# Eighteen ring places for expert weights, two of them shared with the routing tables, in a two-layer decoder step

## The chip, the cores and the metric

The kernel runs on one core of one Trainium2 chip. The metric is the device time of one launch in microseconds; the kernel before has a median of 1427.11 us over 3 runs (1426.06 to 1427.96). All data is float32.

## The reference, cut to what matters

A decoder step of two layers over 512 prompt tokens and 8 sample tokens (520 rows of 1024 elements). Layer 0 attends by stick-breaking, layer 1 by dilated windows over a shared K/V. Each layer ends with the same mixture of experts:

```
def hmoe(h, w_rg, b_rg, w_re, b_re, w_g, w_u, w_d):
    g_idx  = argmax(softmax(h @ w_rg + b_rg))            # one of 4 groups
    top_i  = top_k(softmax(logits of the 8 experts of that group), 2)
    comb   = weights of the two chosen experts, over all 32
    a, u   = einsum('td,edf->tef', h, w_g), einsum('td,edf->tef', h, w_u)
    return einsum('tef,efd->td', silu(a) * u * comb[:, :, None], w_d)
```

Each of the 32 experts has a gate and an up matrix of 1024 x 256 and a down matrix of 256 x 1024, 1 MiB each: 96 matrices, 100.7 MB, in each layer. A token uses two experts, and the kernel reads every expert's weights once per layer.

## The kernel before, in words

The stages follow one another as blocks, in which each engine has its own instruction list and the engines meet through semaphores: attention of layer 0, `moe(0)`, `layer_b` (attention of layer 1: projections from three weight units per key head, then scores, softmax and products), a last stage for the sample rows, `moe(1)`, and a block that adds the experts' rows and stores the output.

**A mixture stage.** TensorE turns the rows of x and multiplies them with the router. VectorE works out the first and second choice of every token, the rank of each token within its expert, and the tables of rows (`lg`, `el`, `tmp`, `run`, `own`, `at`, `who` and others, lines 960 to 990). TensorE reduces the tables to row numbers (semaphore `s_tab`), VectorE writes them to `idx` (L1363), and GpSimd gathers the rows of two experts at a time from DRAM into `xs` (L1464). Beside it VectorE counts tokens beyond the 64 places of an expert and signals `s_over` (L1390); such an overflow has a path of its own after the last pair, which uses some of the tables again. Then come 16 pairs of experts. For each, TensorE multiplies with gate and up (L1034), turns h (L1043, L1045) and multiplies with down (L1052); ScalarE and VectorE copy the results to `ysb`, and GpSimd scatters them to `y_rows` in DRAM (L1470).

**The ring.** A weight matrix is a piece of 1 MiB, 8 KiB on each partition. The pieces are numbered in the order of use: gate and up of expert 2v, gate and up of 2v+1, then the two downs, six for a pair v. They go round a ring of 16 places: the 12 homes of the buffer `slots`, in the order `HOME = (7, 8, ..., 11, 0, ..., 6)`, then two halves of `spare`, `gain_rows`, and a part of `oT`. SyncE (SP) asks for them in its list, L330. The first 12 are asked for as the homes come free, some at the end of the stage before (`load_first`), pieces 12 to 15 after the normed rows are stored and the router is done. From piece 16 on, piece n waits in `used(n - 16)` until TensorE has signalled that the piece which had its place is used.

**After the ring.** In layer 0, SP then asks for the gains `gcol` and for the three weight units of key head 0 of `layer_b` (`load_unit`, L349 to L351): for each unit two parts of 256 KB, in runs of 256 bytes, and one of 1 MB, in runs of 1 KiB, 1.57 MB in all. A unit lies in `slots` from element 14400 on, over homes 7 to 11; `unit_pieces(g)` names the last pieces that used them. All engines leave the stage when SP has seen all scatters landed (`all_stored`).

**The start of `layer_b`.** `rows_back(sp, 0)` and `rows_back(act, 1)` read the 520 rows of the first and of the second choice back from `y_rows` (L1612, 2.13 MB on the queue of SP and as much on that of ScalarE). SP then asks for the head gains `gn` (L1676, L1677). VectorE's list is: clear `tok` (L1979), scale unit 0 by its gains (L1994), ten additions into x, two for each of the five row tiles (L1984), wait for `gn`, two instructions on the gains (L2115, L2116), evict the first two products of unit 0 (L2013, L2014), scale unit 1, and so on; unit 2 is scaled after the second product of unit 1. TensorE warms up (`keep_busy`, L215), turns tile 0 of x when its two additions are done (L1718), multiplies it with unit 0 (L1734), turns tiles 1 and 2, multiplies tile 1, turns tiles 3 and 4, and multiplies tiles 2 and on. The product of tile 2 waits until that of tile 0 has been evicted, since there are two banks.

Of the kernel before, what the change touches and what calls it, by code (L numbers as in the profile page):

```python
# [1 line left out]

# [12 lines left out]
D = 1024  # L15
# [4 lines left out]
NT = len(TILES)  # L20
# [10 lines left out]
NDIL = 3  # L31
KQ = 5 * HD
NG, NE, EPG = 4, 32, 8
FE = D // 4
CAP = 64
NOVER = 2 * TOK // CAP
# [93 lines left out]
def flat(ap):  # L130
    return ap.rearrange("p a b -> p (a b)")


def build(nc, a, outs):
# [11 lines left out]
    with ExitStack() as ctx:  # L146
        def sb(name, shape, dt=F32, to=ctx):
            return to.enter_context(nc.sbuf_tensor(name, shape, dt))
# [38 lines left out]
        gain_rows = sb("gain_rows", [128, 2, D])  # L187
# [111 lines left out]
        PIECE = 2 * D  # L299
        slots = sb("slots", [128, 12 * PIECE])  # L300

        RING = 16
        HOME = (7, 8, 9, 10, 11, 0, 1, 2, 3, 4, 5, 6)

        def home(i):
            return slots[:, PIECE * i:PIECE * i + PIECE]

        def piece(n):

            p, k = n // 6, n % 6  # L310
            return (2 * p + k // 2, k % 2) if k < 4 else (2 * p + k - 4, 2)
# [14 lines left out]
        def load_piece(eng, layer, n, dst):  # L326

            e, k = piece(n)
            sig = s_din[layer][e % 6] if k == 2 else s_gin[layer][e % 6]
            eng.dma_start(dst, weight_rows(layer, e, k)).then_inc(sig, 16)  # L330

        def load_first(eng, layer, homes):
            for i in homes:
                load_piece(eng, layer, HOME.index(i), home(i))

# [10 lines left out]
        def load_unit(sp, j, g):  # L346

            kv = [ds(g * 512 + which * 256 + j * HD, HD) for which in range(2)]
            sp.dma_start(wB[:, g, :, 0:HD], w_kv[:, :, kv[1]]).then_inc(s_unit[g], 16)  # L349
            sp.dma_start(wB[:, g, :, HD:2 * HD], w_kv[:, :, kv[0]]).then_inc(s_unit[g], 16)  # L350
            sp.dma_start(wB[:, g, :, 2 * HD:], w_q[:, :, ds(g * D + j * 256, 256)]).then_inc(s_unit[g], 16)  # L351

        def unit_pieces(g):

            lo, hi = WB + g * KT * UW, WB + (g + 1) * KT * UW
            return [3 * NE - RING + HOME.index(i) for i in range(lo // PIECE, -(-hi // PIECE))]

        phA = ExitStack()
        live.append([])
# [121 lines left out]
        with ExitStack() as ph, nc.Block() as block:  # L481
# [15 lines left out]
            spare = wA[:, 0].rearrange("p k n -> p (k n)")  # L497
# [434 lines left out]
        def moe(layer, norm):  # L932

            L = str(layer)

            def lsem(n):
                return sem(f"{n}_{L}")
# [5 lines left out]
            with ExitStack() as ph, nc.Block() as block:  # L943
                oT_flat = flat(oT)
# [3 lines left out]
                ysb = [sb(f"ysb{w}_" + L, [2 * CAP, D], to=ph) for w in range(2)]  # L948
                spare = sb("spare" + L, [128, 4, D], to=ph)
                xn = [spare[:, w, :] for w in range(NT - 2)] + ysb  # L950
                ring = [home(i) for i in HOME] + [flat(spare[:, 0:2]), flat(spare[:, 2:4]), flat(gain_rows), oT_flat[:, 0:2 * D]]
                over_w = [home(k) for k in range(3)]

                def gate_up_of(w):
# [2 lines left out]
                def down_of(w):  # L957
                    return w.rearrange("p (f d) -> p f d", f=2)

                lg = sb("lg" + L, [128, NT, NG + NE], to=ph)  # L960
                st = sb("st" + L, [128, 9, NT], to=ph)
                g4 = sb("g4" + L, [128, 3, NT, NG], to=ph)
                el = sb("el" + L, [128, NT, NE], to=ph)
                oh = sb("oh" + L, [128, 3, NT, NE], to=ph)
                tmp = sb("tmp" + L, [128, NT, NE], to=ph)
                run = sb("run" + L, [128, NT - 1, NE], to=ph)
                rank = sb("rank" + L, [128, NT * NE], to=ph)
                own = sb("own" + L, [128, 2, NT * NE], to=ph)
                place = sb("place" + L, [128, 2 * NT], to=ph)
                at = sb("at" + L, [128, 2 * NT, CAP], to=ph)  # L970
                who = sb("who" + L, [128, 2 * NT, 2, 2, NE // 2], to=ph)
                idx = sb("idx" + L, [128, 2, NE // 2], I32, to=ph)
                nov = sb("nov" + L, [NE, 2, 128], to=ph)
                ovb = sb("ovb" + L, [128, NE + 1], to=ph)
                far = sb("far" + L, [128, NE], to=ph)
                ovm = sb("ovm" + L, [1, NOVER, NE], to=ph)
                ovf = sb("ovf" + L, [1, NOVER + 1], to=ph)
                oblk = sb("oblk" + L, [128, 2 * NT, NOVER], to=ph)
                owho = sb("owho" + L, [128, 2 * NT, 2, NOVER], to=ph)
                otab = sb("otab" + L, [CAP, 2, NOVER], to=ph)  # L980
                turn_mark = sb("turn_mark" + L, [1, 4], to=ph)
                oidx = sb("oidx" + L, [CAP, 2], I32, to=ph)
# [4 lines left out]
                s_xn, s_tp, s_ev, s_l, s_ex, s_gx, s_oh, s_rk, s_at, s_tab, s_idx, s_nv, s_ob, s_over = (  # L987
                    lsem(n) for n in ("xn_ready", "xn_turned", "xnT_ready", "logits_done", "exp_in",
                                      "exp_ready", "onehot_ready", "ranks_done", "places_ready", "tables_done", "rows_known",
                                      "over_counted", "over_base", "over_known"))  # L990
# [3 lines left out]
                s_xs = [lsem(f"xs_in{w}") for w in range(2)]  # L994
# [101 lines left out]
                @block.sync  # L1096
                def _(sp):
                    open_ring(sp, s_ye + [o_dn, o_ye, o_free])
                    load_first(sp, layer, range(early, early + 2))
                    for t, rows in TILES:  # L1100
                        sp.wait_ge(s_xn, t + 1)
                        sp.dma_start(xn_rows[128 * t:128 * t + rows, :], xn[t][0:rows, :]).then_inc(s_st[0 if t < NT - 2 else NT - 2], 16)
                    load_first(sp, layer, range(early + 2, len(HOME)))
                    sp.wait_ge(s_st[0], 16 * (NT - 2))
                    load_piece(sp, layer, 12, ring[12])
                    load_piece(sp, layer, 13, ring[13])
                    if layer == 0:
                        sp.wait_ge(s_cleared, 16 * (-(-2 * TOK // 128)))
                    load_piece(sp, layer, 14, ring[14])
                    sp.wait_ge(s_l, NT)  # L1110
                    load_piece(sp, layer, 15, ring[15])

                    def used(n):
                        e, k = piece(n)
                        if k == 2:
                            sp.wait_ge(s_dn[e % 2], e // 2 + 1)
                        else:
                            sp.wait_ge(s_gu[e % 2], e // 2 + 1)

                    for n in range(RING, PIECES):  # L1120
                        used(n - RING)
                        load_piece(sp, layer, n, ring[n % RING])
                    if layer == 0:
                        sp.dma_start(gcol[:, 0], a["g_kv"].rearrange("(p t) -> p t", t=KT)).then_inc(s_gcol, 16)
                        sp.dma_start(gcol[:, 1], a["g_attn"][1].rearrange("(p t) -> p t", t=KT)).then_inc(s_gcol, 16)
                        for g in range(NDIL):
                            for n in unit_pieces(g):
                                used(n)
                            load_unit(sp, 0, g)

                    with further_blocks(sp, lambda: all_stored(sp)) as (m, _):
                        e = sp.value_load(over_i[0:1, ds(m, 1)], min_val=0, max_val=NE - 1)
                        sp.wait_ge(o_dn, m + 1)
                        for k in range(3):
                            sp.dma_start(over_w[k], weight_rows(layer, e, k)).then_inc(o_in, 16)
                    all_stored(sp)

                @block.tensor
                def _(pe):
# [56 lines left out]
                    def experts(v):  # L1196
                        n, b = v // 2, v % 2
                        pe.wait_ge(s_xe[b], 2 * n + 2)
                        for q in range(2):
                            e = 2 * v + q  # L1200
                            pe.wait_ge(s_gate_up_in[e % 6], 32 * (e // 6) + 32)
                            gate_up(pe, gate_up_of(ring[(6 * v + 2 * q) % RING]), gate_up_of(ring[(6 * v + 2 * q + 1) % RING]), q,
                                    xsT[b][:, :, CAP * q:CAP * q + CAP], s_gu[q])
# [7 lines left out]
                        for q in range(2):  # L1211
# [3 lines left out]
                            pe.wait_ge(s_down_in[e % 6], 16 * (e // 6) + 16)  # L1215
                            down(pe, down_of(ring[(6 * v + 4 + q) % RING]), q, s_dn[q])

# [333 lines left out]
        def layer_b(norm, next_norm):  # L1551
# [15 lines left out]
            with ExitStack() as ph, nc.Block() as block:  # L1567
# [41 lines left out]
                def rows_back(eng, k, some=TILES):  # L1609
                    for t, rows in some:  # L1610
                        r0 = TOK * k + 128 * t
                        eng.dma_start(yr[0:rows, 2 * t + k, :], y_rows[r0:r0 + rows, :]).then_inc(s_gt[t], 16)  # L1612
# [11 lines left out]
                def _(sp):  # L1624
# [48 lines left out]
                        sp.dma_start(dst[n1:n1 + n2 - 1, :, 1, :], rows("cache_kv_b3", 16)).then_inc(s_past[c], 16)  # L1673

                    rows_back(sp, 0)
                    sp.dma_start(gn[:, 0], a["k_norm_b"].partition_broadcast(128)).then_inc(s_gn, 16)  # L1676
                    sp.dma_start(gn[:, 1], a["q_norm_b"][0].partition_broadcast(128)).then_inc(s_gn, 16)  # L1677
                    sp.wait_ge(norm.s_rstd, NT)
# [812 lines left out]
```

## Time and profile before

| What | Value |
|---|---|
| median of 3 runs | 1427.11 us |
| the profiled execution, its own time | 1429.2 us |
| its span, first to last instruction | 1427.3 us |
| TensorE busy | 1298.7 us (91%) |
| VectorE / ScalarE / GpSimd busy | 44% / 23% / 31% |
| bytes moved by DMA | 319.90 MB, mean 224 GB/s |
| experts of layer 0, of layer 1 | about 385 to 617 us, 1164 to 1399 us |

A busy TensorE is not one at its peak: an instruction that follows closely behind another counts as busy, and `keep_busy` products count too. The page's slices are 35.7 us each. The stretches in which the DMA engines move some 420 GB/s are the two expert stages.

### The profile page before, as it was taken

The numbers are of one execution on the slowest core, as the hardware profiler recorded it, in microseconds if no ns is written. First come the engines' busy times: TensorE is split into PE (matmuls) and PEld (weight loads), VectorE is DVE, ScalarE is ACT, GpSimd is POOL, SyncE is SP. The second block draws the span as 40 slices with busy tenths as digits, with TensorE's granted clock in tenths as the row PEclk, the third lists the DMA queues.
The fourth block names the chain that finished last, engine by engine and source line by source line (L and its number), as shares of the span: only waits on it lengthen the run. The fifth ranks groups of instructions, "written<-read, shape, count | busy, mean of one in ns | idle before, by whom it ended". The sixth has DMA issues, their size and how long they took to land. (4 is left out here: it accounts for less than half of the span.)

```text
span 1427.3 us, 20804 instructions
## 1 busy us (share of the span) xinstructions
PE 1298.7 (91%) x8666; PEld 916.9 (64%) x8666; DVE 625.1 (44%) x940; ACT 323.8 (23%) x642; POOL 443.1 (31%) x381
## 2 busy tenths in 40 slices
PE   7889999999999988879999999999999989997882
PEld 5668878645666644537868868878746646664550
DVE  2277774633522111144457558558446542221114
ACT  3222223312122211112015015015015312221110
POOL 4122325201111111103977576577430101111100
PEclk9999999999999999999999999999999989999996
DMA  9944434263799999991222123022041869999995
GB/s 331 311 134 143 155 112 153 74 267 147 298 420 419 419 420 419 413 297 25 73 61 61 40 53 90 11 53 92 22 121 45 323 272 420 418 419 420 419 394 197
DMA packets 154864, 319.90 MB, mean 224 GB/s; under 512 B 63060, under 2 KB 112100, under 8 KB 130068
## 3 DMA queue, kind: packets, MB, share of 16 engines
q1 hardware_dynamic: 139764, 280.47, 52.6%
q0 software_dynamic: 13824, 33.84, 6.6%
q10 hardware_dynamic: 1184, 4.26, 0.8%
q8 instruction: 70, 1.15, 0.3%
q14 instruction: 22, 0.18, 0.0%
HBM read 300.71 MB, written 34.33 MB: 235 GB/s over the span
## 5 line engine op out<-in xcount | busy, mean ns | idle before, releaser
L1734 PE MATMUL ps<-slots 128*128 128x384 f32 x768 | 261.3, 494 | 0.9 <-ACT slots L1932 0.6
L1734 PEld LDWEIGHTS ps<-slots 128*128 128x128 f32 x768 | 203.1, 270 | 43.4 <-issue 3.0
L1034 PE MATMUL ps<-slots,oT 128*64 128x256 f32 x1536 | 179.8, 390 | 31.7 <-DMA slots<-in_w_up 30.2
L1034 PEld LDWEIGHTS ps<-slots,oT 128*64 128x64 f32 x1536 | 125.7, 140 | 92.0 <-issue 34.4
L583 PE MATMUL ps<-xnT_a,wA 128*128 128x260 f32 (+1 forms) x768 | 172.8, 385 | 3.2 <-DMA wA<-in_w_qkv_a 2.4
L583 PEld LDWEIGHTS ps<-xnT_a,wA 128*128 128x128 f32 x768 | 145.6, 191 | 28.4 <-issue 4.5
L1470 POOL DMA_INDIRECT y_rows<-ysb,idx x32 | 32.1, 1003 | 403.3 <-DVE ysb L1069 403.3
L1060 DVE TENSOR_TENSOR h<-sg,ps 64x256 f32<-64x256 f32 x64 | 26.4, 413 | 262.9 <-ACT sg L1057 262.9
L1052 PE MATMUL ps<-slots,hT 128*64 128x512 f32 x384 | 87.7, 597 | 2.3
L1069 DVE COPY ysb<-ps 64x512 f32<-64x512 f32 x64 | 44.4, 693 | 88.2 <-PE ps L1052 88.2
L1057 ACT ACTIVATE sg<-ps 64x256 f32<-64x256 f32 x64 | 24.4, 381 | 244.5 <-PE ps L1034 244.5
L1954 ACT ACTIVATE slots<-slots,neg 128x128 f32<-128x128 f32 (+1 forms) x192 | 64.1, 417 | 54.8 <-DVE neg L2057 49.2
L912 POOL TENSOR_TENSOR slots<-slots,cst 128x512 f32<-128x512 f32 x32 | 49.4, 1564 | 66.9 <-ACT slots L734 66.8
L891 POOL DMA_INDIRECT slots<-in_cache_kv_a,gidx x32 | 33.3, 1040 | 113.9 <-DVE gain_rows L798 104.4
L2218 POOL TENSOR_TENSOR late_b<-tok 128x1600 f32<-128x1600 f32 x12 | 34.2, 2853 | 105.4 <-DVE tok L2022 105.4
L829 DVE TENSOR_TENSOR_SCAN slots<-slots,gain_rows 128x1024 f32<-128x1024 f32 (+1 forms) x32 | 53.8, 1721 | 27.5 <-POOL slots L912 27.5
L1066 ACT ACTIVATE ysb<-ps 64x512 f32<-64x512 f32 x64 | 37.8, 590 | 108.0 <-PE ps L1052 108.0
L284 PE MATMUL ps<-slots,oT 128*128 128x512 f32 x128 | 58.2, 600 | 1.7 <-PEq L1567 1.3
L1052 PEld LDWEIGHTS ps<-slots,hT 128*64 128x64 f32 x384 | 30.3, 136 | 41.9 <-issue 41.9
L292 DVE TENSOR_TENSOR x<-x,ps 128x512 f32<-128x512 f32 x32 | 21.9, 687 | 77.9 <-PE ps L284 77.9
L2013 DVE TENSOR_SCALAR tok<-ps,rsr 128x320 f32<-128x320 f32 x32 | 17.6, 551 | 85.3 <-PE ps L1734 85.1
L2221 POOL TENSOR_TENSOR late_b<-late_b 128x800 f32<-128x800 f32 (+2 forms) x72 | 53.1, 737 | 5.7
(277 smaller groups left out, 1998.0 us busy)
## 6 DMA issues: line engine op xcount, KB each, us to landing
slots<-in_w_down SPq DMA_DIRECT2D x48, 1024.0 KB, 26.5
slots<-in_w_gate SPq DMA_DIRECT2D x48, 1024.0 KB, 23.2
slots<-in_w_up SPq DMA_DIRECT2D x48, 1024.0 KB, 27.1
wA<-in_w_qkv_a SPq DMA_DIRECT2D x24, 512.0 KB, 4.5
slots<-in_w_q_b SPq DMA_DIRECT2D x12, 1024.0 KB, 7.0
spare<-in_w_gate SPq DMA_DIRECT2D x8, 1024.0 KB, 23.3
spare<-in_w_up SPq DMA_DIRECT2D x8, 1024.0 KB, 26.9
gain_rows<-in_w_gate SPq DMA_DIRECT2D x8, 1024.0 KB, 21.1
```

What stands on the lines that cost most here:

```text
L284: last = nc.tensor.matmul(bank(at + n)[0:TILES[t][1], :], oT[:, m, 128 * t:128 * t + TILES[t][1]], self.w[m][:, 512 * n:512 * n + 512], st ...
L583: last = nc.tensor.matmul(bank(6 + h)[:, 0:half], wA[:, m, k, :], xnT[:, k, half * h:half * h + half], start=(k == 0), stop=(k == KT - 1))
L829: nc.vector.tensor_tensor_scan(P, P, keep[:, at:at + width][:, ::-1], 1.0, ALU.mult, ALU.add).then_inc(s_scan, 1)
L912: nc.gpsimd.tensor_tensor(d, d, C("below").unsqueeze(1).unsqueeze(1).to_broadcast([128, 2, 2, 128]), ALU.mult).then_inc(s_msk, 1)
L1034: last = nc.tensor.matmul(bank(q)[lo:lo + CAP, 0:FE], x[:, k, :], wt[:, k, :], start=(k == 0), stop=(k == KT - 1))
L1052: last = nc.tensor.matmul(bank(4 + q)[CAP * n:CAP * n + CAP, :], hT[:, q, f, :], wt[:, f, 512 * n:512 * n + 512], start=(f == 0), stop=(f ...
L1066: return nc.scalar.activation(ysb[w][CAP * q:CAP * q + CAP, 0:512], bank(4 + q)[0:CAP, :], ACT.Copy)
L1069: return nc.vector.tensor_copy(ysb[w][CAP * q:CAP * q + CAP, 512:D], bank(4 + q)[CAP:2 * CAP, :])
L1734: last = nc.tensor.matmul(bank(i % 2)[:, 0:UW], xT[:, kt, cols], wB[:, g, kt, :], start=(kt == 0), stop=(kt == KT - 1))
L1954: last = nc.scalar.activation(v, v, ACT.Exp, bias=neg[:, 0 if g else 1, b, h:h + 1])
L2218: pool_do(P.tensor_tensor(sq[:, :, :], kq, kq, ALU.mult))
L2221: pool_do(P.tensor_tensor(s4[:, :, :, 0:w], s4[:, :, :, 0:w], s4[:, :, :, w:2 * w], ALU.add))
```

## The change

The ring gets 18 places. The two new ones are the halves of a buffer `scratch` of 2 x 2048 elements per partition, from which a helper `table` cuts ten of the routing tables, which had buffers of their own. Piece 16 takes the first half, after the first gather has landed (`s_xs[0]`) and the tables are reduced (`s_tab`); piece 17 takes the second, after `s_over`. Piece n from 18 on waits for the use of piece n - 18. `HOME` becomes 0 to 11 in order. Unit 0 of `layer_b` is still asked for at the end of `moe(0)`; units 1 and 2 are asked for in `layer_b`, behind `rows_back(sp, 0)` and ahead of `gn`.

```
-        RING = 16
-        HOME = (7, 8, 9, 10, 11, 0, 1, 2, 3, 4, 5, 6)
+        RING = 18
+        HOME = tuple(range(12))
...
-            return [3 * NE - RING + HOME.index(i) for i in range(lo // PIECE, -(-hi // PIECE))]
+            return [max(range(HOME.index(i), 3 * NE, RING)) for i in range(lo // PIECE, -(-hi // PIECE))]
...
-                ring = [home(i) for i in HOME] + [flat(spare[:, 0:2]), flat(spare[:, 2:4]), flat(gain_rows), oT_flat[:, 0:2 * D]]
+                scratch = sb("scratch" + L, [128, 2, PIECE], to=ph)
+                ring = [home(i) for i in HOME] + [flat(spare[:, 0:2]), flat(spare[:, 2:4]), flat(gain_rows), oT_flat[:, 0:2 * D],
+                                                  scratch[:, 0], scratch[:, 1]]
+                def table(half, rows, *shape):      # the next free stretch of that half of scratch, in that shape
...
-                lg = sb("lg" + L, [128, NT, NG + NE], to=ph)
+                lg = table(0, 128, NT, NG + NE)
...              (so too el, tmp, run, at, who in half 0; own, nov, ovm, oblk, owho in half 1)
                     load_piece(sp, layer, 15, ring[15])
+                    sp.wait_ge(s_xs[0], 16)
+                    sp.wait_ge(s_tab, 1)
+                    load_piece(sp, layer, 16, ring[16])
+                    sp.wait_ge(s_over, 1)
+                    load_piece(sp, layer, 17, ring[17])
...
-                        for g in range(NDIL):
-                            for n in unit_pieces(g):
-                                used(n)
-                            load_unit(sp, 0, g)
+                        for n in unit_pieces(0):
+                            used(n)
+                        load_unit(sp, 0, 0)
...
                     rows_back(sp, 0)
+                    load_unit(sp, 0, 1)
+                    load_unit(sp, 0, 2)
                     sp.dma_start(gn[:, 0], a["k_norm_b"].partition_broadcast(128)).then_inc(s_gn, 16)
```

## Rows read from the trace of the kernel before

**Rows 1.** The page: span, and GB/s in 40 slices of it.
```profile
span 1427.3 us, 20804 instructions
...
GB/s 331 311 134 143 155 112 153 74 267 147 298 420 419 419 420 419 413 297 25 73 61 61 40 53 90 11 53 92 22 121 45 323 272 420 418 419 420 419 394 197
```

**Rows 2.** Windows: stretch, length, busy by engine, then PEclk, DMA share, GB/s.
```profile
390.00:604.00 214.00, 193.41 (x1395) 125.84 (x1393) 41.52 (x89) 45.04 (x89) 27.57 (x28) 0.99 1.01 417
1172.00:1386.00 214.00, 191.72 (x1381) 124.63 (x1378) 41.30 (x89) 44.90 (x89) 27.26 (x27) 0.99 1.01 419
384.00:390.00 6.00, 5.28 (x49) 3.60 (x49) 0.55 (x2) 2.75 (x4) 0.99 (x1) 1.00 0.18 51
1160.00:1170.00 10.00, 8.27 (x41) 5.37 (x43) 0.00 (x0) 2.48 (x3) 0.99 (x1) 0.54 0.11 30
```

**Rows 3.** Waits of TensorE, 460 to 620 us: total, times, longest, in us.
```profile
PE ps L1034 <- DMA slots<-in_w_up: 15.3, 10, 2.5
```

**Rows 4.** Timeline, layer 0, 383 to 403 us: start, duration, engine, line, what.
```profile
383.20 0.74 PE L1021 MATMUL ps<-cst,xs 128*128 128x128 f32 x2 [0.68 <-DMA xs<-xn_rows,idx]
...
383.97 0.17 DVE L1390 CAST over_i<-ovf 1x17 int32<-1x17 f32 x1
...
389.16 0.80 SPq L330 DMA_DIRECT2D slots<-in_w_down  x2
...
402.07 0.82 SPq L330 DMA_DIRECT2D slots<-in_w_down  x2
```

**Rows 5.** Timeline, layer 1, 1158 to 1171 us.
```profile
1158.34 0.16 DVE L1390 CAST over_i<-ovf 1x17 int32<-1x17 f32 x1
1161.04 0.56 PEld L1021 LDWEIGHTS ps<-cst,xs 128*128 128x128 f32 x2 [4.98 <-DMA xs<-xn_rows,idx]
...
1170.35 0.81 SPq L330 DMA_DIRECT2D slots<-in_w_down  x2
```

**Rows 6.** Timeline, end of `moe(0)` and start of `layer_b`, 595 to 655 us.
```profile
595.05 16.03 SPq L350 DMA_DIRECT2D slots<-in_w_kv_b  x1
...
607.93 3.67 PE L1034 MATMUL ps<-spare,oT 128*64 128x256 f32 x32 [1.19 <-DMA spare<-in_w_up]
...
618.25 0.97 POOL L1470 DMA_INDIRECT y_rows<-ysb,idx  x1 [13.54 <-DVE ysb L1069]
...
627.81 2.25 SPq L1612 DMA_DIRECT2D slots<-y_rows  x5
...
627.85 8.14 PE L215 MATMUL ps<-cst 128*128 128x512 f32 x12 [6.70 <-PEq L943]
...
629.17 3.42 DVE L1994 TENSOR_TENSOR slots<-slots,gcol 128x1024 f32<-128x1024 f32 x2
...
634.53 7.89 DVE L1984 SCALAR_TENSOR_TENSOR x<-slots,wts,x 128x1024 f32<-128x1024 f32 x6 [1.93 <-DMA slots<-y_rows]
...
637.19 1.16 PE L1718 MATMUL ps<-cst,x 128*128 128x128 f32 x8 [1.19 <-DVE x L1984]
...
642.88 5.22 DVE L1984 SCALAR_TENSOR_TENSOR x<-slots,wts,x 128x1024 f32<-128x1024 f32 x4 [0.47 <-DMA slots<-y_rows]
...
648.14 0.35 DVE L2115 TENSOR_SCALAR late_b<-late_b 128x192 f32<-128x192 f32 x1
...
649.25 0.55 DVE L2013 TENSOR_SCALAR tok<-ps,rs 128x320 f32<-128x320 f32 x1
649.72 0.28 DVE L2014 TENSOR_SCALAR vo<-ps,rs 128x64 f32<-128x64 f32 x1
...
654.17 10.59 PE L1734 MATMUL ps<-slots 128*128 128x384 f32 x32
```

**Rows 7.** Timeline, end of `moe(1)` and the last block.
```profile
1401.12 0.97 POOL L1470 DMA_INDIRECT y_rows<-ysb,idx  x1 [13.03 <-DVE ysb L1069]
1405.71 2.58 SPq L1523 DMA_DIRECT2D yr<-y_rows  x5
...
1410.70 7.89 DVE L1544 SCALAR_TENSOR_TENSOR x<-yr,wts,x 128x1024 f32<-128x1024 f32 x6 [10.41 <-DMA yr<-y_rows]
```

**Rows 8.** Windows around weight units, columns as in rows 2.
```profile
727.00:733.00 6.00, 6.00 (x32) 3.66 (x31) 2.26 (x4) 0.00 (x0) 5.61 (x6) 1.00 0.96 258
628.00:642.00 14.00, 12.46 (x30) 5.86 (x31) 11.74 (x9) 2.06 (x3) 1.39 (x2) 0.81 1.01 372
```

More of the change, by code:

```diff
@@ L1 @@
+import math
 from contextlib import ExitStack, contextmanager
@@ L950, in moe @@
                 xn = [spare[:, w, :] for w in range(NT - 2)] + ysb
-                ring = [home(i) for i in HOME] + [flat(spare[:, 0:2]), flat(spare[:, 2:4]), flat(gain_rows), oT_flat[:, 0:2 * D]]
+                scratch = sb("scratch" + L, [128, 2, PIECE], to=ph)
+                ring = [home(i) for i in HOME] + [flat(spare[:, 0:2]), flat(spare[:, 2:4]), flat(gain_rows), oT_flat[:, 0:2 * D],
+                                                  scratch[:, 0], scratch[:, 1]]
+                taken = [0, 0]
+                def table(half, rows, *shape):
+                    lo = taken[half]
+                    taken[half] = lo + math.prod(shape)
+                    assert taken[half] <= PIECE
+                    dims = "abcd"[:len(shape)]
+                    return scratch[0:rows, half, lo:taken[half]].rearrange(
+                        f"p ({' '.join(dims)}) -> p {' '.join(dims)}", **dict(zip(dims, shape)))
                 over_w = [home(k) for k in range(3)]
@@ L958, in down_of @@
                     return w.rearrange("p (f d) -> p f d", f=2)
-                lg = sb("lg" + L, [128, NT, NG + NE], to=ph)
+                lg = table(0, 128, NT, NG + NE)
                 st = sb("st" + L, [128, 9, NT], to=ph)
                 g4 = sb("g4" + L, [128, 3, NT, NG], to=ph)
-                el = sb("el" + L, [128, NT, NE], to=ph)
+                el = table(0, 128, NT, NE)
                 oh = sb("oh" + L, [128, 3, NT, NE], to=ph)
-                tmp = sb("tmp" + L, [128, NT, NE], to=ph)
-                run = sb("run" + L, [128, NT - 1, NE], to=ph)
+                tmp = table(0, 128, NT, NE)
+                run = table(0, 128, NT - 1, NE)
                 rank = sb("rank" + L, [128, NT * NE], to=ph)
-                own = sb("own" + L, [128, 2, NT * NE], to=ph)
+                own = table(1, 128, 2, NT * NE)
                 place = sb("place" + L, [128, 2 * NT], to=ph)
-                at = sb("at" + L, [128, 2 * NT, CAP], to=ph)
-                who = sb("who" + L, [128, 2 * NT, 2, 2, NE // 2], to=ph)
+                at = table(0, 128, 2 * NT, CAP)
+                who = table(0, 128, 2 * NT, 2, 2, NE // 2)
                 idx = sb("idx" + L, [128, 2, NE // 2], I32, to=ph)
-                nov = sb("nov" + L, [NE, 2, 128], to=ph)
+                nov = table(1, NE, 2, 128)
                 ovb = sb("ovb" + L, [128, NE + 1], to=ph)
                 far = sb("far" + L, [128, NE], to=ph)
-                ovm = sb("ovm" + L, [1, NOVER, NE], to=ph)
+                ovm = table(1, 1, NOVER, NE)
                 ovf = sb("ovf" + L, [1, NOVER + 1], to=ph)
-                oblk = sb("oblk" + L, [128, 2 * NT, NOVER], to=ph)
-                owho = sb("owho" + L, [128, 2 * NT, 2, NOVER], to=ph)
+                oblk = table(1, 128, 2 * NT, NOVER)
+                owho = table(1, 128, 2 * NT, 2, NOVER)
                 otab = sb("otab" + L, [CAP, 2, NOVER], to=ph)
```

## The prediction, made before the changed kernel was timed

> **What bounds the kernel now.** I read the page first, for where the DMA engines are full. The 40 slices show two stretches at 420 GB/s, slices 12 to 17 and 34 to 38, and mostly far less elsewhere [rows 1]. These are the two expert stages, and the reader is to see that they run at one rate whatever TensorE does. I then asked for windows: 417 and 419 GB/s at a share of 1.01 over 214 us in either layer, and ahead of each a hole, 51 GB/s between 384 and 390 us and 30 GB/s between 1160 and 1170 us [rows 2]. In the hole the ring is full: all 16 pieces have landed, and the next is asked for only when the first expert is done, at 389.16 us [rows 4] and at 1170.35 us [rows 5].
>
> TensorE would be faster than the DMA. While it still lives on the pieces in stock, the wait for the same place of the pair is passed 12.91 us apart (389.16 and 402.07 us [rows 4]). Six pieces are 6.29 MB, at 417 GB/s 15.1 us. So the stock of 16 runs out, and from 460 us on TensorE waits for up matrices, 15.3 us in ten waits on those in `slots` alone [rows 3], the last one at 607.93 us, for the very last gate and up pair [rows 6]. An expert stage therefore ends at: the moment the DMA begins again after the hole, plus the bytes still to come, plus a tail of fixed work. I looked last at that tail, in the timeline of both layers [rows 6, 7], because the change moves DMAs out of it in one layer, and the other shows it without them.
>
> **The ring, in both layers.** Piece 16 may now go when the first gather has landed and the tables are reduced. TensorE starts on that gather's rows at 383.20 us [rows 4] and at 1161.04 us [rows 5]. Piece 17 may go after the overflow count, 383.97 plus 0.17 us [rows 4] and 1158.34 plus 0.16 us [rows 5]. Both conditions come before the first expert is done, by 5 us in layer 0 and by 9 us in layer 1. Two pieces take 2 x 1.049 MB / 417 GB/s = 5.0 us, so they just fit the hole of layer 0 and easily that of layer 1. At 389.16 us SP asks for pieces 18 and 19 where it asked for 16 and 17, and so on: each request goes out when it did before and is for a piece two further on. The saturated stretch has 78 pieces to bring in place of 80, the same gathers and scatters, and ends 5.0 us sooner. Layer 0: -5.0 us. Layer 1: -5.0 us.
>
> Does TensorE become the bound before that? Its waits for weights add up to over 15 us [rows 3], of which 5 go, and the last wait is at the end of the stretch, so the DMA still decides. The bounds of this term: -5.4 us for a layer, if the DMA also starts sooner by what is left of the gap, and -2.5 us, if only one piece fits in the hole.
>
> The Trainium skill ("DMA: Bandwidth & Descriptors", Specifications) gives about 358 GB/s as the limit of HBM for one core. By it two pieces would be worth 5.9 us a layer; the 417 and 419 GB/s of rows 2 speak against it here, and the sum goes by these.
>
> The tables' move to `scratch` changes no shape of a VectorE or TensorE instruction; I cost it at nothing. The order of `HOME` decides which of the first pieces comes first; all 16 are in before the first expert starts, since the DMA is idle by then [rows 2], so it costs nothing either. The two new waits of SP stand in front of `used(0)`, and are over before it, as shown; behind them SP has only weight requests.
>
> **The end of `moe(0)`.** The last scatter goes out at 618.25 us, and all engines go on at 627.81 us, 9.56 us later [rows 6]. In layer 1, with no weight units behind the experts, it is 1401.12 to 1405.71 us, 4.59 us [rows 7]. In between SP asks in layer 0 for units 1 and 2, whose 3.1 MB share the DMA engines with the scatter. After the change only unit 0 is left. Its first parts were blocked in SP's queue for 16.03 us, until 611.08 us, when the weights had nearly all landed [rows 6]; that block moves along with the weights, so unit 0 should be in when the scatter starts or shortly after. I take the value of layer 1: -5.0 us. Bounds: 0 (unit 0 disturbs the scatter as all three did) and -5.0 us.
>
> **The rows back.** VectorE is free for the additions 4.8 us after the stage's start S (629.17 + 3.42 - 627.81 [rows 6]); its first addition starts at S + 6.72 us, waiting for rows, while the same rows are there at S + 4.99 us in layer 1 [rows 7]. Behind the change no rest of unit 2 is in the queue ahead of the rows. -1.7 us (bounds 0 and -1.9, where VectorE itself is the bound). TensorE turns tile 0 at S + 9.38 us now, after two additions of 1.32 us (7.89 / 6 [rows 6]); then at 5.0 + 2.6 = S + 7.65 us. Its warm-up of 12 products takes 8.14 us here, after 6.70 us of idle time [rows 6], and the granted clock of these 14 us is 0.81 in the mean [rows 8], so some 5 us at 1.2 GHz and the rest at 2.4; that idle time shrinks to 1.7 us, so I expect no drop, and if it does drop, 0.5 us of the gain is lost.
>
> **The head gains, later.** Here the change gives something back. `gn` now stands in SP's queue behind the rows (4.26 MB with those of ScalarE's queue) and behind units 1 and 2. Rows at 417 GB/s from about S + 1.5: done at S + 11.7 us. A unit alone moves in 6 us at 258 GB/s [rows 8], 5.4 us of which are in use at a share near 1; two are 10.8 us, and `gn` lands at about S + 23 us, if the rows start no later than here (372 GB/s over the 14 us from the start of the stage, unit 2 included [rows 8]). Now it is used at 648.14 us, S + 20.3 us, with no wait [rows 6]. Behind VectorE's wait for it stand the two gain instructions and the eviction of the first product, 1.9 us in all (648.14 to 649.72 + 0.28 [rows 6]). TensorE wants that eviction for the product of tile 2, 16.98 us after it turns tile 0 (637.19 to 654.17 [rows 6]), so at S + 24.6 us. 23 + 1.9 = 24.9 us: nearly even. Since the small runs of the units may move slower behind the rows, I take +1.5 us, range 0 to +4. Unit 1 is needed at once after (its scaling stands behind the second eviction) and has landed by then; unit 2 is needed some 24 us later. From there TensorE is busy without a gap through the projections, so the rest of `layer_b` moves as a whole.
>
> **The sum.** -5.0 (ring, layer 0) - 5.0 (scatter) - 1.7 (rows) + 1.5 (gains) - 5.0 (ring, layer 1) = -15.2 us. On the profiled execution (1429.2 us, span 1427.3) that gives 1414.0 us; the median is 2.1 us below it, so 1411.9 us. The likeliest case's own range is 1409.0 to 1415.5.
>
> **The rivals.**
> 1. The tail gives nothing: unit 0 still collides with the last scatter, and the rows start no faster. For it: one unit is a third of the bytes, its first parts are stuck until the weights are in, and the scatter follows 7 us after. Against it: the request for its last part comes some 7 us before the scatter. Then -10 + 1.5 = -8.5 us, 1418.6 us; half of it gives 1415.
> 2. The gains come late: SP is blocked again for some 16 us in asking for the small runs of a unit (as at 595.05 us [rows 6]), now with `gn` behind it. Against it: there ten weight pieces were in the queue, here two megabytes of rows. If one block adds 12 us to `gn`, the sum is -16.7 + 12 = -4.7 us, 1422.4 us.
> 3. The other side: both new units block for 16 us each. `gn` then lands near S + 51, VectorE and with it the product of tile 2 stand for some 28 us, and the sum is -16.7 + 28 = +11 us, 1438 us. It decides from a delay of `gn` of 17 us beyond S + 23 on. Only the one row of 16.03 us speaks for it.
> 4. The ring doesn't do what it says: the two pieces are in early, but another thing than the bytes sets the end of the expert stages, such as SP's requests. Against it: 1.01 of share throughout [rows 2]. Then only the tail is left, -5.2 us, 1421.9 us.
>
> **How the numbers follow.** My forecast 0.63, rival 1 0.20, rival 2 0.06, rival 3 0.03, rival 4 0.05, anything else 0.03. The range of 8 in 10 takes in the forecast's own range and most of rival 1: 1408.5 to 1418.5 us. A measurement of this kernel tells about 0.2% (2.9 us) from no change. All cases but rival 3 and half of the rest are faster by more: 0.94 faster, 0.02 the same, 0.04 slower.
>
> **What would show it.** Ring: between 384 and 390 us and between 1160 and 1170 us the DMA moves 2 MB more, and the last gate and up of layer 0 starts 5 us sooner, while the rate stays at 417 to 419 GB/s. Scatter: 4.6 us from its start to the rows' request, in place of 9.56. Rows: first addition 5.0 us after that. Gains: a wait of VectorE on `late_b` ahead of L2115 of about 4 us, and a wait of TensorE of about 1.5 us ahead of the product of tile 2. The prediction is wrong if the expert stages shorten by less than 4 us each, or if VectorE's wait for the gains is over 8 us.

## The result

The changed kernel takes 1416.22 us (median of 6 runs, 1414.26 to 1421.42), the kernel before beside it 1427.53 us (6 runs). The ratio is 0.9916, with a 95% interval of 0.9901 to 0.9931: 11 to 12 us faster. The forecast was 1411.9 us in a range of 1408.5 to 1418.5; the direction and the range held, and of the 15.2 us forecast about 4 did not come. The likeliest case's own range, 1409.0 to 1415.5, was missed by 0.7 us. The profiled execution of the changed kernel took 1415.32 us, with a span of 1413.4 us.

The first view is the one that carried the sum: windows of the changed kernel, columns as in rows 2: the two holes, the two saturated stretches, and the first 14 us of `layer_b`.

```profile
382.00:388.00 6.00, 5.26 (x51) 3.41 (x51) 0.41 (x1) 2.59 (x4) 0.99 (x1) 1.00 0.91 373
387.00:600.00 213.00, 194.61 (x1423) 127.97 (x1419) 41.97 (x90) 45.32 (x91) 28.35 (x28) 1.00 1.01 417
1152.00:1162.00 10.00, 8.59 (x45) 5.59 (x47) 0.00 (x0) 2.53 (x4) 0.99 (x1) 0.56 0.61 238
1163.00:1377.00 214.00, 196.97 (x1415) 129.66 (x1411) 41.61 (x90) 45.44 (x90) 28.34 (x28) 0.98 1.01 415
615.50:629.50 14.00, 11.41 (x35) 5.83 (x36) 12.15 (x9) 2.06 (x3) 2.44 (x2) 1.00 0.97 329
```

Where 51 and 30 GB/s moved in the holes [rows 2], 373 and 238 do now, and the rate behind them is the same 417 and 415. The hole of layer 0 is full; that of layer 1 is filled by half.

The waits of TensorE, 457 to 618 us (total, times, longest), show that the weights still decide: 11.4 us on up matrices in `slots`, where it was 15.3 [rows 3].

```profile
PE ps L1048 <- DMA slots<-in_w_up: 11.4, 8, 2.2
PE ps L1048 <- DMA spare<-in_w_up: 3.0, 2, 1.7
```

The timeline of layer 0 and of the start of `layer_b` follows, which answers to rows 4 and 6. S is again the start of `layer_b`, 615.57 us here. (TensorE's gate and up are line 1048 here, L1034 before; the request for a piece is L331.)

```profile
380.70 1.37 SPq L331 DMA_DIRECT2D scratch<-in_w_down  x2
...
386.69 0.33 SPq L331 DMA_DIRECT2D slots<-in_w_gate  x1
...
588.24 15.65 SPq L351 DMA_DIRECT2D slots<-in_w_kv_b  x1
...
600.96 3.67 PE L1048 MATMUL ps<-slots,oT 128*64 128x256 f32 x32 [1.19 <-DMA slots<-in_w_up]
...
611.28 0.98 POOL L1488 DMA_INDIRECT y_rows<-ysb,idx  x1 [13.22 <-DVE ysb L1083]
...
615.57 2.39 SPq L1630 DMA_DIRECT2D slots<-y_rows  x5
...
615.61 5.39 PE L216 MATMUL ps<-cst 128*128 128x512 f32 x12 [1.43 <-PEq L944]
...
619.45 9.46 SPq L352 DMA_DIRECT2D slots<-in_w_q_b  x1
620.47 2.61 DVE L2004 SCALAR_TENSOR_TENSOR x<-slots,wts,x 128x1024 f32<-128x1024 f32 x2
623.14 1.16 PE L1738 MATMUL ps<-cst,x 128*128 128x128 f32 x8 [2.13 <-DVE x L2004]
...
635.24 1.00 SPq L1696 DMA_DIRECT2D late_b<-in_k_norm_b  x1
...
640.77 0.35 DVE L2135 TENSOR_SCALAR late_b<-late_b 128x192 f32<-128x192 f32 x1 [5.93 <-DMA late_b<-in_q_norm_b]
...
642.68 13.61 PE L1754 MATMUL ps<-slots 128*128 128x384 f32 x32 [2.49 <-DVE vo L2034]
```

The scatter is 4.29 us ahead of the next stage, as in layer 1, in place of 9.56. The first addition comes at S + 4.90 us, the turn of tile 0 at S + 7.57. Then the last two rows: VectorE waits 5.93 us for the head gains, TensorE 2.49 us for the eviction behind them, and the product that it waited with takes 13.61 us in place of 10.59 [rows 6]. Windows of 2 us from 640 us on say why:

```profile
640.00:642.00 2.00, 0.18 (x2) 0.09 (x1) 1.17 (x3) 2.00 (x5) 0.54 (x2) 0.99 0.01 3
642.00:644.00 2.00, 1.32 (x2) 0.84 (x3) 2.00 (x5) 0.49 (x2) 0.98 (x3) 0.50 0.00 0
644.00:646.00 2.00, 2.00 (x4) 1.01 (x3) 2.00 (x2) 0.00 (x0) 0.00 (x0) 0.50 0.13 1
646.00:648.00 2.00, 2.00 (x5) 1.05 (x4) 0.60 (x1) 0.00 (x0) 0.00 (x0) 0.50 0.00 0
648.00:650.00 2.00, 2.00 (x7) 1.17 (x6) 0.00 (x0) 0.00 (x0) 0.00 (x0) 0.80 0.00 0
```

TensorE had been idle from 640.18 us, and its granted clock is 0.50, 1.2 GHz, from 642 to beyond 648 us.

Cut at the same eight places, the profiled executions compare as follows (in us; A to the end of the first gate and up of layer 0, B from there to its last scatter, C to the start S of `layer_b`, D to the turn of tile 0, E to the product of the sample rows with unit 0, F to the end of the first gate and up of layer 1, G to its last scatter, H to the end of the span):

| | before | changed | ring only | units only | gains first |
|---|---|---|---|---|---|
| A | 389.16 | 386.70 | 386.24 | 386.76 | 387.82 |
| B ring, layer 0 | 229.09 | 224.58 | 224.40 | 229.28 | 224.36 |
| C scatter | 9.56 | 4.29 | 8.65 | 4.29 | 4.30 |
| D rows back | 9.38 | 7.57 | 9.90 | 7.62 | 7.55 |
| E gains | 27.49 | 33.08 | 27.49 | 31.67 | 27.49 |
| F | 505.67 | 505.73 | 504.95 | 505.50 | 505.04 |
| G ring, layer 1 | 230.77 | 226.04 | 226.17 | 230.94 | 225.98 |
| H | 26.18 | 25.41 | 25.60 | 25.84 | 25.56 |

B, C, D, E and G are the change: -4.5, -5.3, -1.8, +5.6, -4.7 us, together -10.7. A and H hold nothing that it touches ahead of the two new pieces; they differ by 2.5 and 0.8 us between these executions, and so the two spans lie 13.9 us apart where the medians say 11.3. E is not the same in every execution either: the changed kernel had 33.08 us in this one and 30.32 us in a second one, for a reason that comes below.

### The profile page after: what moved, and what is told of

It is laid out like the page before. It is cut to its first block and busy times, and to the rows that moved or that the text cites. A ratio compares the mean times of both kernels' runs of the same rounds, so it can differ in the third digit from the quotient of the medians.

```text
span 1413.4 us, 20804 instructions
## 1 busy us (share of the span) xinstructions
PE 1299.7 (92%) x8666; PEld 919.5 (65%) x8666; DVE 625.1 (44%) x940; ACT 323.8 (23%) x642; POOL 443.6 (31%) x381
## 5 line engine op out<-in xcount | busy, mean ns | idle before, releaser
L1754 PE MATMUL ps<-slots 128*128 128x384 f32 x768 | 264.3, 499 | 3.4 <-DVE vo L2034 2.5
L1048 PE MATMUL ps<-slots,oT 128*64 128x256 f32 x1408 | 162.7, 387 | 24.1 <-DMA slots<-in_w_up 21.9
L1048 PEld LDWEIGHTS ps<-slots,oT 128*64 128x64 f32 x1408 | 115.7, 140 | 77.0 <-issue 28.5
L1066 PE MATMUL ps<-slots,hT 128*64 128x512 f32 x352 | 80.4, 597 | 1.9
L830 DVE TENSOR_TENSOR_SCAN slots<-slots,gain_rows 128x1024 f32<-128x1024 f32 (+1 forms) x32 | 53.8, 1721 | 27.5 <-POOL slots L913 27.5
L2246 POOL TENSOR_TENSOR late_b<-late_b,cst 128x25 f32<-128x25 f32 x12 | 52.4, 4363 | 0.9
```

The source lines that it names most:

```text
L830: nc.vector.tensor_tensor_scan(P, P, keep[:, at:at + width][:, ::-1], 1.0, ALU.mult, ALU.add).then_inc(s_scan, 1)
L1048: last = nc.tensor.matmul(bank(q)[lo:lo + CAP, 0:FE], x[:, k, :], wt[:, k, :], start=(k == 0), stop=(k == KT - 1))
L1066: last = nc.tensor.matmul(bank(4 + q)[CAP * n:CAP * n + CAP, :], hT[:, q, f, :], wt[:, f, 512 * n:512 * n + 512], start=(f == 0), stop=(f ...
L1754: last = nc.tensor.matmul(bank(i % 2)[:, 0:UW], xT[:, kt, cols], wB[:, g, kt, :], start=(kt == 0), stop=(kt == KT - 1))
L2246: pool_do(P.tensor_tensor(ss, ss, C("mhalf").unsqueeze(2).to_broadcast(shape), ALU.pow))
```

## The experiments

Each kernel was timed beside the kernel before, in three sets of four. The first eight kernels ran on one chip, the last four on another; ratios are to the kernel before in the same set.

**One part at a time.** Theory A: the parts add up as in the table. The rivals: the ring is all of it, or bytes are not the bound at all.

```
 ring only:   RING = 18 and HOME = 0..11, but in moe(0)
-                        for n in unit_pieces(0):
-                            used(n)
-                        load_unit(sp, 0, 0)
+                        for g in range(NDIL):
+                            for n in unit_pieces(g):
+                                used(n)
+                            load_unit(sp, 0, g)
 units only:  RING = 16 and the old HOME, units 1 and 2 asked for behind rows_back, ahead of gn
```

> Eighteen places, but all three weight units asked for at the end of the first expert stage, as before. Theory A (terms add up as in the traces: ring -4.5 and -4.7 us, the tail as before): -9.2 us, 1418.3 us, ratio 0.9936. Theory B (the ring alone explains the whole change): same as the changed kernel, 0.9916. Theory C (bytes do not set the end of the expert stages): 1.000.

Measured: 0.9928 (0.9914 to 0.9941). The ring is worth 10 us, B and G of the table (-4.7 and -4.6 us), and not the whole change. "Bytes do not set the end" is out.

> Sixteen places in the old order, only units 1 and 2 asked for later, ahead of the gains. Theory A: -5.3 (scatter) - 1.8 (rows) + 5.5 (gains and clock) = -1.6 us, ratio 0.9989. Theory B (the late gains cost only the 1.5 us forecast, and 3 us of the shortfall were elsewhere): -5.5 us, 0.996. If the gains cost more than the scatter gives, it is slower than before.

Measured: 0.9971 (0.9961 to 0.9981), 4 us, between the two theories' numbers. The profile has both halves: C and D fall by 7.0 us, and E rises by 4.2 us. The product of tile 2 took 12.28 us, 1.7 more than before, behind a wait of 1.39 us. The other 1.0 us or so of E lies further ahead: the clock also fell at the turn of tile 0 (see the last section).

**The gains ahead of the units.** The suspected cost taken away, alone and with the ring:

```
                     rows_back(sp, 0)
-                    load_unit(sp, 0, 1)
-                    load_unit(sp, 0, 2)
                     sp.dma_start(gn[:, 0], ...).then_inc(s_gn, 16)
                     sp.dma_start(gn[:, 1], ...).then_inc(s_gn, 16)
+                    load_unit(sp, 0, 1)
+                    load_unit(sp, 0, 2)
```

> The changed kernel with the two requests for the head gains put ahead of units 1 and 2. In the changed kernel VectorE waited 5.93 us for the gains, TensorE then 2.49 us for the first eviction, and the product that followed took 13.61 us in place of 10.59, at a clock of 0.5 at first. Theory A (the gains' place in the queue caused both): that wait goes, and the time falls by 2.5 + 3.0 = 5.5 us, to about 0.988 of the kernel before (1410.7 us). Theory B (the units behind the rows are slow for everybody, so something else is late next, scaling unit 1 above all): the wait moves to unit 1 and less than 2 us is won, 0.990 to 0.992.

Measured: 0.9892 (0.9878 to 0.9907), median 1413.47 us. By the ratios that is 3.4 us better than the changed kernel, where 5.5 was expected. In its timeline VectorE goes from the last addition to the gains with no wait, E is 27.49 us as before the change, and no other wait took its place:

```profile
619.12 0.36 SPq L1694 DMA_DIRECT2D late_b<-in_k_norm_b  x1
...
635.12 0.35 DVE L2135 TENSOR_SCALAR late_b<-late_b 128x192 f32<-128x192 f32 x1
...
639.92 3.42 DVE L2014 TENSOR_TENSOR slots<-slots,gcol 128x1024 f32<-128x1024 f32 x2
```

> As the units-only kernel, with the gains asked for ahead of units 1 and 2. Theory A: -5.3 - 1.8 = -7.1 us, ratio 0.9950, and 5.5 us below the units-only kernel. Theory B (another wait takes the place of the gains'): within 2 us of the units-only kernel.

Measured: 0.9953 (0.9939 to 0.9966), against 0.9971 for the units-only kernel in the same set: 2.6 us, less than the 5.5 expected. In the traces E is 31.67 us with late gains and 28.47 with early ones, 3.2 us apart.

The changed and the gains-first kernel were run once more on the second chip, side by side.

> The changed kernel once more, on the chip of the three that follow, as their base: ratio 0.9916 within 0.15%. If it moves with the chip, only differences within this set are used.

Measured: 0.9913 (0.9898 to 0.9928), median 1416.06 us. The result repeats. But in this execution the clock did not fall in the wait ahead of tile 2: that wait was 1.64 us, and the product behind it took 10.59 us. It had fallen earlier, at the turn of tile 0, which takes 1.35 us here in place of 1.16, and the first product behind it 6.02 us in place of 5.40; the granted clock is 0.50 from 626 to 628 us. TensorE was done with the turns at S + 25.8 us and not at S + 24.6, so it also had less to wait for the eviction.

```profile
624.23 1.35 PE L1738 MATMUL ps<-cst,x 128*128 128x128 f32 x8 [2.21 <-DVE x L2004]
...
627.08 6.02 PE L1754 MATMUL ps<-slots 128*128 128x384 f32 x16
...
642.12 0.35 DVE L2135 TENSOR_SCALAR late_b<-late_b 128x192 f32<-128x192 f32 x1 [6.82 <-DMA late_b<-in_q_norm_b]
...
644.02 10.59 PE L1754 MATMUL ps<-slots 128*128 128x384 f32 x32 [1.64 <-DVE vo L2034]
```

> The gains-first kernel once more, beside the changed kernel. Theory A (late gains cost the wait and the clock behind it): 3 to 5.5 us below the changed kernel, with no wait for the gains in VectorE's list. Theory B (the first comparison was a difference of chips): within 1 us of it.

Measured: 0.9895 (0.9877 to 0.9913), median 1411.35 us against 1416.06. Its five times lie in two groups, three at 1411.1 to 1411.4 us and two at 1416.5 to 1416.6, so the median hangs on one of them. The three comparisons of late with early gains agree in sign and give 2.6 us (0.9971 and 0.9953), 3.4 us (0.9916 and 0.9892, not timed side by side) and 2.6 us by ratio or 4.7 by median here. In the traces E differs by 3.2, 5.6 and 1.7 us in the same pairs. The intervals of each pair overlap, so it is the series, and the wait that is seen to go in every trace, that shows it: late gains cost about 3 us in the mean, and 5.6 in the one execution in which the clock fell in that wait and not before it.

**How far behind is too far.**

```
                     load_unit(sp, 0, 1)
+                    sp.dma_start(gn[:, 0], ...)
+                    sp.dma_start(gn[:, 1], ...)
                     load_unit(sp, 0, 2)
```

> The changed kernel with the gains asked for between units 1 and 2. Theory A (the gains land when what is ahead of them in the queue has landed; one unit ahead instead of two, some 5.5 us less): they land at about S + 19.6 us in place of S + 25.1, VectorE waits under 1 us, TensorE does not wait, and the time is that of the gains-first kernel. Theory B (the queue's order is not what holds the gains, but the load of the engines until unit 2 has landed): they land after S + 22.7 us and TensorE still waits.

Measured: 0.9906 (0.9891 to 0.9921), between its two neighbours and not told from either by time. The trace decides: the gains are used at S + 20.66 us (S is 616.12 us here) after a wait of 1.60 us, 1.1 us later than expected, and TensorE does not wait. One unit less ahead brings them 4.9 us earlier than in the repeat of the changed kernel.

```profile
636.78 0.35 DVE L2135 TENSOR_SCALAR late_b<-late_b 128x192 f32<-128x192 f32 x1 [1.60 <-DMA late_b<-in_q_norm_b]
...
642.08 10.59 PE L1754 MATMUL ps<-slots 128*128 128x384 f32 x32
```

The gains land with what stands ahead of them, whenever SP asks. Behind the rows alone (gains first) they were asked for at S + 2.6 and 3.0 us and landed at S + 13.5 and 14.1; behind unit 1, which landed at S + 19.9, they were asked for at S + 13.6 and 14.6 and landed at S + 19.0 and 20.6; behind unit 2, which landed at S + 24.6 in the changed kernel, they were asked for at S + 19.7 and 20.7 and landed at S + 24.6 and 25.1. So the time from request to landing is no property of the request. Its median over the two requests is 12.5 us in the kernel before (first line) and 4.6 in the changed one (second):

```profile
DMA to landing us min/median/max: 12.2/12.5/12.7
...
DMA to landing us min/median/max: 4.4/4.6/4.9
```

In the changed kernel the DMA engines were kept at work all that time. From 618 to 626 us they moved 395 to 418 GB/s. From there to 640 us, with the last rows and the short runs of the units, it was 280 GB/s in the mean, at a share that never fell below 0.94 in windows of 2 us. Some of them, columns as in rows 2:

```profile
624.00:626.00 2.00, 1.66 (x7) 0.72 (x6) 1.93 (x3) 1.67 (x2) 0.00 (x0) 1.00 1.02 416
626.00:628.00 2.00, 2.00 (x8) 1.21 (x7) 1.97 (x2) 0.40 (x2) 1.44 (x2) 1.00 1.09 332
628.00:630.00 2.00, 2.00 (x7) 1.17 (x7) 0.95 (x2) 0.00 (x0) 1.00 (x1) 1.00 1.34 185
634.00:636.00 2.00, 2.00 (x8) 1.21 (x7) 0.84 (x1) 1.83 (x3) 1.53 (x3) 1.00 1.12 190
636.00:638.00 2.00, 2.00 (x8) 1.21 (x7) 0.00 (x0) 0.00 (x0) 0.65 (x2) 1.00 0.94 309
```

**The clock by itself.** Both kernels are the changed one with warm-up products in TensorE's wait; the wait of VectorE stays.

```
+                    pe.wait_ge(s_xc, 4)      # second kernel: 3
+                    keep_busy(6, 6)          # second kernel: keep_busy(3, 6)
                     for c in range(2, NCHUNK):
                         project(0, 0, c)
```

> The changed kernel with six warm-up products of TensorE (2.6 us at 2.4 GHz) put into its wait for the first eviction, into a bank that is free. The wait itself stays. Theory A (3.0 of the 5.5 us given back are the clock, which fell in the 2.5 us of idle time): the product of tile 2 and what follows run at full clock, -3 us against the changed kernel, 1413.2 us, ratio 0.990. Theory B (the clock would fall anyway, or the slow product has another cause, such as VectorE's scaling beside it): no gain, or up to 0.5 us lost.

Measured: 0.9948 (0.9928 to 0.9967), slower than the changed kernel. I had the size wrong: a call is two passes, and six calls are 12, 5.42 us. The timeline shows the product at full clock, 10.48 us, but begun at 648.37 us, 4.1 us after the eviction (644.04 + 0.28 us). E is 33.97 us, more than in any trace with late gains and no warm-up products.

```profile
643.12 5.42 PE L216 MATMUL ps<-cst 128*128 128x512 f32 x12
...
644.04 0.28 DVE L2036 TENSOR_SCALAR vo<-ps,rs 128x64 f32<-128x64 f32 x1
...
648.37 10.48 PE L1754 MATMUL ps<-slots 128*128 128x384 f32 x32
```

> The changed kernel with three warm-up calls (six passes, 2.7 us at 2.4 GHz) in TensorE's wait for the first eviction, which starts at once and fits in the 2.5 us of that wait. In the first warm kernel six calls took 5.42 us, the clock stayed up and the product took 10.48 us, but it began 4.1 us after the eviction. Theory A (the idle time lets the clock fall, at a cost of 1.7 to 3.0 us): the product starts at S + 27.1 to 27.5 us, takes 10.5 us, and the kernel is 1.5 to 3 us below the changed kernel. Theory B (the drop costs nothing in the end, being made up behind it): equal to the changed kernel.

Measured: 0.9898 (0.9883 to 0.9913), against 0.9913 for the changed kernel beside it: 2 us, inside the intervals. The product took 10.48 us and began at S + 28.5, 1.4 us after the eviction and a microsecond later than expected. Its E is 31.15 us against 30.32 of the changed kernel beside it, so the trace shows no gain. In both warm kernels TensorE was at work through the wait and the product ran at 2.4 GHz, which fits the idle time as the cause of the drop. Two traces do not prove it, since the product of the repeat ran at 2.4 GHz without them; what the warm-up is worth stays open.

**The places themselves.**

```
 seventeen (on the gains-first kernel):   RING = 17, and no piece 17 asked for early
```

> The gains-first kernel with a ring of 17: only piece 16 is early. Theory A (each place is worth its bytes, 2.3 to 2.5 us a layer, as long as it fits in the hole): +4.6 us against the gains-first kernel, ratio about 0.9913. Theory B (the first extra piece takes the whole gain, the second collides with gathers): within 1 us of the gains-first kernel.

Measured: 0.9909 (0.9887 to 0.9931), against 0.9892 and 0.9895 with 18 places. The trace is sharper: B is 226.83 us and G 228.27, about half way between 16 and 18 places in both layers. Each place is worth 2.3 to 2.5 us a layer, its bytes. The kernel also shows an accident: with 17 places home 7 last holds piece 92, so unit 0 is asked for only after the last gate and up, and the scatter takes 6.16 us in place of 4.3.

```profile
608.36 0.55 SPq L350 DMA_DIRECT2D slots<-in_w_kv_b  x1
...
621.07 2.67 SPq L1628 DMA_DIRECT2D slots<-y_rows  x5
```

```
 home order (on the changed kernel):      HOME = (7, 8, 9, 10, 11, 0, 1, 2, 3, 4, 5, 6)
```

> The changed kernel with the old order of the homes (7 to 11, then 0 to 6) in the ring of 18. Theory A (all pieces of the first round have landed before the first expert, so their order is worth nothing): as the changed kernel, 0.9916, within 0.1%. Theory B (the order matters at the end of the first expert stage, where the units' homes come free at another time): the last parts of unit 0 land later and the scatter is disturbed again, up to +5 us.

Measured: 0.992 (0.9902 to 0.9938), as the changed kernel. Unit 0 is asked for at 600.07 us here, 11.4 us ahead of the last scatter (611.45), and C is 4.30 us. So the order is worth nothing, and a request for unit 0 may come as late as that. At 6.5 us ahead of the scatter, in the kernel of 17, the scatter took 1.9 us longer; that the late request is the cause rests on this one trace.

**The wait for the gather.**

```
 on the gains-first kernel:
-                    sp.wait_ge(s_xs[0], 16)
                     sp.wait_ge(s_tab, 1)
                     load_piece(sp, layer, 16, ring[16])
```

> The gains-first kernel without the wait for the first gather ahead of piece 16, which then goes when the tables are reduced, some 4 us earlier in layer 0 and 9 us in layer 1. Theory A (the stage's end hangs on the first expert's end, from which the requests start again): the gather shares the engines with a piece in layer 0 and lands 1 to 2.5 us later, so the kernel is 1 to 3 us slower; in layer 1 piece 16 comes behind a queue that is still full, and the gather is slowed there too. Theory B (bytes alone count): as the gains-first kernel, or up to 1 us faster.

Measured: 0.9932 (0.9914 to 0.9949) against 0.9892: 5.7 us slower, about twice the most that I expected. From the first store of the normed rows to the end of the first gate and up of layer 0 it is now 39.8 us (352.12 to 391.93), where it is 35.4 with the wait (352.43 to 387.82). Only piece 16 is asked for earlier, by 6.1 us counted from the first store; piece 17 still waits for the overflow count. The first two gathers share the engines with piece 16 and take 7.1 and 6.2 us from request to landing, in place of 5.0 and 4.8. TensorE waits 3.15 us for the first, in place of 1.08; the next windows show the rest of the cost, the clock:

```profile
383.62 0.85 PE L1035 MATMUL ps<-cst,xs 128*128 128x128 f32 x2 [3.15 <-DMA xs<-xn_rows,idx]
```

```profile
384.00:386.00 2.00, 1.96 (x9) 1.55 (x8) 0.00 (x0) 0.60 (x2) 0.00 (x0) 0.50 0.93 385
386.00:388.00 2.00, 1.36 (x8) 0.78 (x10) 0.00 (x0) 1.87 (x2) 0.99 (x1) 0.50 0.12 45
388.00:390.00 2.00, 2.00 (x14) 1.15 (x12) 0.00 (x0) 0.00 (x0) 0.00 (x0) 0.54 0.44 127
390.00:392.00 2.00, 2.00 (x22) 1.32 (x20) 0.00 (x0) 0.07 (x1) 0.00 (x0) 1.00 0.03 10
```

The pieces are in early, the hole moves behind them (45, 127 and 10 GB/s), and the requests start again with the end of the first expert, which is later. Having the bytes sooner is worth nothing there; being done with the first expert is. B stays at 224.46 us. In layer 1 a gather takes up to 10.2 us beside piece 16, and nothing is lost: F is 505.83 us, against 505.04 and 505.75 in the two traces of the gains-first kernel.

The fastest version is the gains-first kernel: 0.9892 and 0.9895 of the kernel before in its two sets, 1413.47 and 1411.35 us. Its E is 27.49 us in one trace, as before the change, and 28.60 in the other, where the clock fell at the turn of tile 0.

## Why the prediction was right, and where it was not

*The ring.* Right in mechanism and nearly in size: forecast -5.0 us in each layer, measured -4.5 and -4.7 in the trace, about 10 us in the ring-only kernel. Pieces 16 and 17 went out in the holes, every later request is for a piece two further on, and the rate did not change. Each place alone gave its bytes (17 places). That the ring does not do what it says (rival 4) is out.

*The order of the homes and the tables in one buffer, at nothing.* The order is shown to be worth nothing. The tables' move was not tried alone; VectorE's busy time is 625.1 us before and after.

*The scatter.* -5.3 us for a forecast of -5.0. The row taken from layer 1, where no units follow, was the right price: 4.59 us there, 4.29 here. The 16 us for which SP is held up in asking for unit 0 moved along, as written. Rival 1 (unit 0 disturbs the scatter) did not come, but the kernel of 17 places may show a part of it, 1.9 us, where unit 0 is asked for late.

*The rows back.* -1.8 us for -1.7. The warm-up took 5.39 us after an idle time of 1.43 us, with no drop of the clock, as forecast. What the forecast lacked is the next wait. The warm-up now ends 2.75 us sooner and the turn of tile 0 comes only 1.8 us sooner, so TensorE waits 2.13 us ahead of it and not 1.19. In ten of the twelve traces of kernels with units 1 and 2 moved, the clock fell there, and where the gains are early E is 28.5 to 28.6 us instead of 27.49. The profiled execution of the changed kernel is one of the two without it, which was luck.

*The gains: this is the step that was mis-sized.* The forecast had them land at S + 23 us, VectorE waiting about 4 us and TensorE 1.5, and took +1.5 us in a range of 0 to +4. They landed at S + 25.1 us and were used at S + 25.2 us, the waits were 5.93 and 2.49 us, and the term is +5.6 us in the profiled execution, outside the range. Over the four traces with late gains and no warm-up products it is +4.2 us in the mean, with the clock at the turn of tile 0 in it; by the times of the pairs the late gains alone cost about 3.

Two things were missing. First, the bytes: I had the rows at 417 GB/s and then each unit in 5.4 us, as it moves alone, so that both would be in at S + 22.5 us. Behind and beside the rows they moved slower, 280 GB/s for everything from 626 us on, and unit 2 landed at S + 24.6 us. SP came to the gains only at S + 19.7 us, having been held up for 9.46 us in asking for the last part of unit 1, but that did not set their time, since they landed within 0.6 us of unit 2, and in the other kernels with what stood ahead of them too. Of rival 2 the hold of SP came, 9.46 us where it had 16; its 12 us on the gains did not. Second, I had put the clock into the sum at the start of `layer_b`, where TensorE idles for 1.4 us, and not in the wait that the change adds. Where it falls there, it costs as much as the wait or more: 3.0 us against 2.49, and 1.7 us against 1.39 and 1.25.

*Behind that.* F is 505.67 us before and 505.73 after, so what was left at that point was there at the end. The remaining 0.5 us or so between the sum of -10.7 us and the medians is within what A and H differ from one execution to the next.

The forecast's single number was 4.3 us low. The start of `layer_b` (E) makes up 2.7 us of it, the ring 0.8; the scatter and the rows gave 0.4 us more than forecast, and the rest, 1.2 us, is not placed. The median lies in the part of the stated range that was added for rival 1. Rival 1 did not come, so it is in part luck that the range held.

## What to carry to other kernels

Where a stage lives on a saturated DMA, a buffer more is worth its bytes, as long as the hole in which it is filled is there, and only if its request does not delay what starts the stage. When a transfer is moved on a queue, go through everything that now stands behind it there, and reckon the bytes ahead at the rate at which they move together, not at the rate of each alone. A small transfer with a consumer goes ahead of large ones without. And where a change adds a wait to TensorE or lengthens one, price the clock along with it.

## What the runs showed of the hardware that I had not expected

In waits of nearly the same length TensorE's clock falls or does not. Before the product of tile 2 the waits were 2.49, 1.39, 1.25 and 1.64 us (changed, units only, home order, changed again), and the product took 13.61, 12.28, 12.28 and 10.59 us. The same holds ahead of the turn of tile 0: eight turning products took 1.16 us in the gains-first kernel, behind a wait of 2.12 us, and 1.97 in the kernel with gains first and 16 places, behind one of 2.19 us, with a granted clock of 0.58 in the 2 us around them. D does not see this, but E is then 28.5 us where it is 27.5. When the gains are late as well, a part of this is not paid twice: TensorE comes later to the wait for the eviction and waits less. That is why E was 30.32 us in the repeat of the changed kernel, with this drop alone, and 33.08 us in the first, with the other alone.

SP can be held up for 5 to 16 us in asking for a transfer of short runs: 15.65 and 5.67 us for 256 KB in runs of 256 bytes, 9.46 us for 1 MB in runs of 1 KiB, where the same two lines also took 0.79 and 0.67 us. Everything behind it in its list waits too. Neither case here shows a cost: nothing stands behind unit 0 at the end of `moe(0)`, and at the start of `layer_b` the DMA engines stayed at work meanwhile.
